# Wide side products from contiguous forms, and the fourth weight sum on GpSimd, in a transformer kernel on one core

## The chip, the cores and the metric

The kernel runs on one core of a Trainium2 chip. The metric is the device time in microseconds (us) of one execution. Engines: PE is TensorE's matmul side and PEld its weight load, DVE is VectorE, ACT is ScalarE, POOL is GpSimd, SP is SyncE, which issues the loads of the weights.

## The reference

Two blocks of two layers each work on one sequence of 512 tokens with 1024 features, in fp32. They contain attention mixers and six gated feed-forward networks, and the change lies in the first half of these:

```python
gate, up = jnp.split(h @ w_ffn_in[l], 2, axis=-1)      # first block
f = (jax.nn.silu(gate) * up) @ w_ffn_out[l]
...
return (jax.nn.silu(h @ wg) * (h @ wu)) @ wd           # second block
```

`h` is x after an RMS norm, 512 x 1024; gate and up have 2816 columns, which are 22 tiles of 128.

## The kernel before

**Precision.** Each fp32 operand is split into a high part (rounded to fp32r by ScalarE) and a low part (the rest). A product is three matmuls: high weight by high data, high weight by low data, low weight by high data. Weights are stationary, the data moves through, 512 columns of tokens at most.

**Order of work.** Weights come in units of 128 x 1024 floats through a ring of four slots (`w_raw`, with `w_hi` and `w_lo` beside it). Each engine runs its own queue, written out by hand; semaphores with counted values join them. In most stages ScalarE makes a unit's high part, GpSimd the low part (`split`, L757 to L764).

**The pair stage.** Each of the six networks does its first 5 gate and 5 up tiles in the plain way (`PLAIN` is 10) and then 17 pairs of a gate tile and an up tile (`PAIRS_ST`) by Strassen's method in Winograd's form: the pair's weights are a 2 x 2 matrix of blocks (gate and up by the halves of the features, `A11`, `A12`, `A21`, `A22`), the data one of 2 x 2 "forms" of 4 x 256 columns a partition (`B11`, `B21`, ... and the combinations `T1` to `T4`). A pair needs seven products instead of eight, and four sums of weight blocks (`S1` to `S4`, each 128 x 512):

- S1 = A21 + A22 (`first_sum`, L1833), S2 = S1 + A11 (`second_sum`, L1837), S4 = S2 + A12 (`fourth_sum`, L1841), S3 = A11 + A21 (`third_sum`, L1845); the signs that the method needs lie in the forms and in `hidden`. All four are VectorE's additions, line L1825.
- The high parts of blocks and sums are ScalarE's (`high`, L1146), the low parts VectorE's (`low`, L1818). The low part of a sum is written over the sum.

**TensorE's queue for pair p** (`paired_units`, L2785 to L2851): the products A11 x B11, S1 x T1, A22 x T4 of the pair before (`fourth`), S2 x T2, A12 x B21, S4 x B22, S3 x T3, counted on `st_prod`. Each is 8 matmuls with the high weight (L2806, L2808) and 4 with the low weight (L2813), all 256 columns wide. Only A12 x B21 of pairs 1 to 15 (`st.wide(p)`) is different: B21's high and low parts lie in `mvh` in such a way that one matmul takes both, 512 columns as 2 pieces of 256 that are two tiles apart (L2803), so that 4 matmuls do for 8. Its halves land in the two halves of `left_bank`, and must be added later.

**VectorE's queue for pair p** (`period`, L1872 to L1932, with q = p + 1) in order: low part of A11 of pair q, S1, the product of SiLU(gate) and up of the pair before (`hidden`, L1854), low part of A22, S2, low parts of S1 and S3 together (128 x 1024), low part of A12; then, after product six and ScalarE's third copy, the gate's additions: L1917 (out of both banks, 512 columns), S4's sum, L1921 (the right half of `left_bank`, 256 columns); then `last_half` (L1869), S3's sum, low parts of S2 and S4 together.

**ScalarE's queue** (`period`, L1180): copies of partial results out of PSUM (L1189, `fifth_copy` L1163, `sixth_copy` L1172), the high parts in the order in which TensorE needs them, SiLU (L1168) after the gate's additions, and then S4's high part. In pair 0 the high part of form T3 (`form_high`, L1143) stands ahead of the fifth copy, and T4 behind it; T3's high part waits until VectorE has split B21 (`form_low`, L1814). TensorE waits for the fifth copy before it begins A12 x B21.

**GpSimd** has nothing to do during the pairs. Its next work are the splits of the stage that follows (`splits`, L779).

**SyncE** (`pairs`, L715) loads a pair's two units when the counts of `st_sum` and `st_lo` say that the slots are free.

Of the kernel before, what the change touches and what calls it, by code (L numbers as in the profile page):

```python
# [32 lines left out]
S = 512  # L33
# [104 lines left out]
def program(nc, x_in, p_in, weights, cols_in, gmlp_in, dist_in, ident_in, rotary_in,  # L138
# [4 lines left out]
    with ExitStack() as ctx:  # L143
# [434 lines left out]
        class Pairs:  # L578


            def __init__(self, name):
                L, i = lin[name], ffn_no(name)
                self.u0, self.e0, self.i = L.u0, L.e0, i
                self.f0 = FFN[name] + PLAIN // 2
                self.g0 = L.e0 + PLAIN
                self.sum0, self.hi0, self.lo0 = 4 * PAIRS_ST * i, (7 * PAIRS_ST + 4) * i, (7 * PAIRS_ST + 4) * i
                self.prod0, self.copy0, self.u_0 = (7 * PAIRS_ST + 3) * i, 3 * PAIRS_ST * i, PAIRS_ST * i
                self.slot0 = L.u0 + PLAIN
                self.form0 = 7 * i
                self.loads0 = (16 * ((PAIRS_ST + 1) // 2) * i, 16 * (PAIRS_ST // 2) * i)  # L590
                m = 4 if name[0] == "a" else 0
                wide = lambda t: t.rearrange("p a (b c) -> p (a b) c", c=S // 2)
                late = [wide(t[:, m + j:m + j + 2, :]) for t in (mvh, mvl) for j in (0, 2)]
                self.both = {B21: mvh[:, m:m + 4, :].rearrange("p (j a) (b c) -> p j (a b) c", j=2, c=S // 2)}

                def homes(y, big, scr):
                    ys = [wide(y[:, 2 * j:2 * j + 2, :]) for j in range(1, 4)]
                    tail = [wide(big[:, FT + 2 * j:FT + 2 * j + 2, :]) for j in range(3)]
                    return {B11: ys[0], T3: ys[1], T1: ys[2], B21: tail[0], B22: tail[1], T2: tail[2],
                            T4: wide(scr[:, 6:8, :])}  # L600

                self.full, self.low = homes(y, big, scr), homes(y_r, big_r, scr_r)
                tabs = [tab_r[:, 1024 * j:1024 * (j + 1)].rearrange("p (a c) -> p a c", c=S // 2) for j in range(2)]
                pair = lambda t: t.rearrange("p (s a) (b c) -> p s (a b) c", s=2, c=S // 2)
                self.normal = [pair(y[:, 2:6, :]), pair(big[:, FT:FT + 4, :])]
                self.high = {B11: wide(scr_r[:, 8:10, :]), T1: tabs[0], T2: tabs[1]}
                self.high.update({B21: late[0], B22: late[2], T3: self.low[B21], T4: self.low[B22]})
                self.low.update({B21: late[1], B22: late[3]})

            def block(self, of, form, n=1):  # L610
                at = (2 * (self.slot0 % RING) + form) % 8
# [22 lines left out]
            def wide(self, p):  # L634

                return 0 < p < PAIRS_ST - 1
# [119 lines left out]
        def _(pool):  # L756
# [19 lines left out]

            done = [0]

            def splits(until):  # L779

                u0 = done[0]
                turns = (until - u0) // RING
                if turns:
                    with pool.Fori(0, turns) as t:
                        for j in range(RING):
                            split(t * RING + u0 + j, (u0 + j) % RING)
                for u in range(u0 + turns * RING, until):
                    split(u, u % RING)
                done[0] = until
# [195 lines left out]
        def _(act):  # L985
# [143 lines left out]
            def ffn_in(name):  # L1129
# [50 lines left out]
                def period(t, p):  # L1180
                    q = p + 1
                    product_done(t, p, 1)
                    if p == 0:
                        act.wait_ge(hidden_ready, st.f0 - 1)
                    elif p == 1:
                        act.wait_ge(hidden_ready, st.f0)
                    else:
                        ge(act, bank_free, t * 2 + st.g0 + p - 1)
                    nc.scalar.activation(parted[:, (p + 1) % 2, 0:S // 2], st.chain_bank(p)[:, 0:S // 2],  # L1189
                                         ACT.Copy).then_inc(st_copy, 1)  # L1190
                    if p == 1:
                        silu_pair(t, 0)
                        sum_high(t, 1, S4)
                    if p == 0:
                        form_high(T3)
                        fifth_copy(t, p)
                        form_high(T4)
                    else:
                        sum_high(t, p, S3)
                    if q < PAIRS_ST:  # L1200
                        raw_high(t, q, A11, 0, 0)
                    if p:
                        fifth_copy(t, p)
                    if p == 0:
                        sixth_copy(t, p)
                    if p == 1:
                        product_done(t, p, 3)
                        raw_high(t, p, A22, 1, 1)
                    if q < PAIRS_ST:
                        sum_high(t, q, S1)  # L1210
                    else:
                        down_cast(2)
                    if p > 1:
                        product_done(t, p, 3)
                    if p != 1:
                        raw_high(t, p, A22, 1, 1, 1 if q < PAIRS_ST else 3)
                    if p:
                        sixth_copy(t, p)
                    if q < PAIRS_ST:
                        sum_high(t, q, S2)  # L1220
                        product_done(t, p, 5)
                        raw_high(t, q, A12, 0, 1)
                    else:
                        down_cast(3)
                        down_high(name, 0)
                    if p:
                        silu_pair(t, p)
                        if q < PAIRS_ST:
                            sum_high(t, q, S4)
                    if q == PAIRS_ST - 1:  # L1230
                        act.wait_ge(mv_free, st.i + 1)
                        down_cast(0)
                        down_cast(1)
# [397 lines left out]
        def _(dve):  # L1631
# [150 lines left out]
            def ffn_in(name):  # L1782
# [41 lines left out]
                def summed(t, q, form, a, b):  # L1824
                    nc.vector.tensor_tensor(st.sum(form), a, b, ALU.add).then_inc(st_sum, 1)  # L1825

                def sum_ready(t, q, n):
                    dve.wait_ge(st_sum, t * 8 + st.sum0 + 4 * q + n)
# [9 lines left out]
                    sum_ready(t, q, 1)  # L1838
                    summed(t, q, S2, st.sum(S1), st.raw(q, 0, 0))

                def fourth_sum(t, q):  # L1841
                    sum_ready(t, q, 2)
                    summed(t, q, S4, st.sum(S2), st.raw(q, 0, 1))

                def third_sum(t, q):  # L1845
                    summed(t, q, S3, st.raw(q, 0, 0), st.raw(q, 1, 0))

# [24 lines left out]
                def period(t, p):  # L1872
# [41 lines left out]
                    if st.wide(p):  # L1914
                        halves = lambda a: a.rearrange("p (j c) -> p j c", j=2)
                        g, b = halves(g1[:, p % 2, :]), halves(parted[:, (p + 1) % 2, :])
                        nc.vector.tensor_tensor(g, st.sides(p, 0), b, ALU.add).then_inc(gate_begun, 1)  # L1917
                        fourth_sum(t, q)
                        dve.wait_ge(gate_begun, t * 2 + (PAIRS_ST - 2) * st.i + p)
                        gate = g1[:, p % 2, 0:S // 2]  # L1920
                        nc.vector.tensor_tensor(gate, st.left_bank(p)[:, S // 2:S], gate, ALU.add).then_inc(bank_free, 1)  # L1921
                    else:
                        nc.vector.tensor_tensor(g1[:, p % 2, :], st.side_bank(p)[:, :], parted[:, (p + 1) % 2, :],
                                                ALU.add).then_inc(bank_free, 1)
                        if more:
                            fourth_sum(t, q)
                    if p:
                        last_half(t, p)
                    if more:
                        third_sum(t, q)  # L1930
                        high_ready(t, q, 7)
                        low(S2, st.sum(S2, 2), 2, 2)  # L1932
# [643 lines left out]
        def _(pe):  # L2576
# [208 lines left out]
            def paired_units(name):  # L2785
# [3 lines left out]
                def product(t, p, bank, weight, n_hi, n_lo, form, begin, more=1):  # L2789
# [6 lines left out]
                    high, low = st.high[form], st.low[form]  # L2796
                    both = st.both[form] if form in st.both and st.wide(p) else None
                    if both is not None:
                        whole = bank
                    for k in range(4):  # L2800
                        w = st.hi(weight)[:, k * P:(k + 1) * P]
                        if both is not None:
                            nc.tensor.matmul(whole.rearrange("p (j c) -> p j c", j=2), w, both[:, :, k, :],  # L2803
                                             start=(begin and k == 0), stop=False, skip_group_check=True)
                            continue
                        nc.tensor.matmul(bank, w, high[:, k, :], start=(begin and k == 0), stop=False,  # L2806
                                         skip_group_check=True)
                        nc.tensor.matmul(bank, w, low[:, k, :], start=False, stop=False, skip_group_check=True)  # L2808
                    pe.wait_ge(st_lo, t * 14 + st.lo0 + 7 * p + n_lo)
                    bank = bank[:, 0:S // 2] if both is not None else bank  # L2810
                    for k in range(4):
                        w = st.lo(weight)[:, k * P:(k + 1) * P]
                        last = nc.tensor.matmul(bank, w, high[:, k, :], start=False, stop=(k == 3),  # L2813
# [12 lines left out]
                def period(t, p):  # L2826
                    chained, left, right = st.chain_bank(p)[:, 0:S // 2], st.side_bank(p)[:, 0:S // 2], st.right(p)
                    fifth_at, third_at = right, right
                    if st.wide(p):
                        left = st.left_bank(p)[:, :]  # L2830
                    if p == 1:
                        pe.wait_ge(bank_free, st.g0)
                    elif p:
# [872 lines left out]
```

## Time and profile before

| | us |
|---|---|
| median of 3 runs | 3206.0 |
| lowest and highest run | 3204.86 and 3206.11 |
| the profiled execution | 3205.18 |
| its span, first to last instruction | 3203.4 |
| TensorE busy | 3154.3 |
| VectorE busy | 2038.4 |
| ScalarE busy | 1497.2 |
| GpSimd busy | 1096.5 |

The span is that of the profiled execution, and the time of that execution is 1.8 us longer. The granted clock of TensorE was 0.999 of full speed over the span. Busy times are sums over instructions of one engine; on VectorE, ScalarE and TensorE an instruction can start before the one ahead of it has ended, so two starts are a better measure of a step than a duration. Starts are in us from the span's start.

### The profile page before, as it was taken

What the parts mean: (1) busy time and instruction counts of PE and PEld (TensorE: products, weight loads), DVE (VectorE), ACT (ScalarE), POOL (GpSimd) and SP (SyncE); (2) the same over time, 40 slices, a digit from 0 to 9 for tenths busy, and PEclk for the clock granted to TensorE, in tenths of its full rate; (3) what the DMA queues carried; (4) which work ended last, traced back from release to release, by engine and by line L of the source; (5) the groups of instructions that cost most, each with busy time, mean ns of one, the idle gap of its engine ahead of it and who ended that gap; (6) DMA issues with size and microseconds to landing.
All of it is one profiled execution on the core that took longest, in us unless ns stands there. A gap on an engine that the chain in (4) does not pass through costs nothing.

```text
span 3203.4 us, 53431 instructions
## 1 busy us (share of the span) xinstructions
PE 3154.3 (98%) x18866; PEld 2726.9 (85%) x18866; DVE 2038.4 (64%) x3193; ACT 1497.2 (47%) x2696; POOL 1096.5 (34%) x635
## 2 busy tenths in 40 slices
PE   9999999999999999999999999999999999999999
PEld 7678998786689987899888778998899887789987
DVE  4748884558488845888445247874698443348854
ACT  4655552547555524555333434552355333335542
POOL 5533014765340146500465341014400453350034
PEclk9999999999999999999999999999999999999999
DMA  4112332221123322222422122232222322122231
GB/s 158 53 47 86 106 117 99 86 103 53 47 85 106 112 103 81 80 105 92 154 92 86 53 73 79 105 118 98 79 101 92 130 93 71 61 86 92 105 119 66
DMA packets 82432, 294.25 MB, mean 92 GB/s; under 512 B 9035, under 2 KB 11467, under 8 KB 82028
## 3 DMA queue, kind: packets, MB, share of 16 engines
q1 hardware_dynamic: 80944, 286.06, 25.4%
q10 hardware_dynamic: 1340, 6.23, 0.5%
q8 instruction: 92, 1.51, 0.2%
q14 instruction: 56, 0.46, 0.0%
HBM read 290.15 MB, written 2.10 MB: 91 GB/s over the span
## 4 chain that ended last, share of the span: by engine, by line
PE 90%; DVE 4%; issue 2%; POOL 2%; ACT 2%; DMA 0%; SPq 0%; POOLq 0%; DVEq 0%; ACTq 0%
PE bank L2581 17%; PE bank L2582 17%; PE bank L2583 17%; PE bank L2813 10%; PE bank L2806 9%; PE bank L2808 9%; PE bank L2803 3%; PE bank L3215 1%; PE bank L3195 1%; POOL w_lo L762 1%; DVE w_lo L1818 1%; PE bank L3302 1%; POOL diag L897 1%; PE bank L3057 1%; PE bank L3337 0%
## 5 line engine op out<-in xcount | busy, mean ns | idle before, releaser
L762 POOL TENSOR_TENSOR w_lo<-w_raw,w_hi 128x1024 fp32r<-128x1024 f32 (+1 forms) x334 | 790.5, 2375 | 1852.2 <-ACT w_hi L991 1808.1
L2581 PE MATMUL bank<-mvh,w_hi 128*128 128x512 f32 (+1 forms) x2774 | 1056.9, 381 | 10.1 <-DVE mvl L1727 2.9
L2583 PE MATMUL bank<-mvh,w_lo 128*128 128x512 f32 (+1 forms) x2774 | 1034.5, 373 | 0.0
L2582 PE MATMUL bank<-mvl,w_hi 128*128 128x512 f32 (+1 forms) x2774 | 1033.8, 373 | 0.0
L991 ACT ACTIVATE w_hi<-w_raw 128x1024 fp32r<-128x1024 f32 x333 | 350.9, 1058 | 799.7 <-PE bank L2583 759.3
L2581 PEld LDWEIGHTS bank<-mvh,w_hi 128*128 128x128 f32 x2774 | 522.5, 188 | 135.3 <-issue 35.2
L2583 PEld LDWEIGHTS bank<-mvh,w_lo 128*128 128x128 f32 x2774 | 522.3, 188 | 93.6
L2582 PEld LDWEIGHTS bank<-mvl,w_hi 128*128 128x128 f32 x2774 | 523.1, 189 | 84.4 <-issue 0.2
L1992 DVE TENSOR_TENSOR mvl<-big,mvh 128x512 fp32r<-128x512 f32 x108 | 255.3, 2364 | 327.8 <-ACT mvh L1280 327.8
L1146 ACT ACTIVATE w_hi<-w_lo_as 128x512 fp32r<-128x512 f32 x408 | 254.7, 626 | 202.8 <-DVE w_lo_as L1825 202.8
L2808 PE MATMUL bank<-y_as,w_hi 128*128 128x256 f32 x1224 | 306.9, 283 | 0.0
L1818 DVE TENSOR_TENSOR w_lo<-w_lo_as,w_hi 128x1024 fp32r<-128x1024 f32 (+1 forms) x216 | 251.1, 1165 | 42.7 <-ACT w_hi L1146 33.5
L1818 DVE TENSOR_TENSOR w_lo<-w_raw,w_hi 128x512 fp32r<-128x512 f32 x306 | 210.8, 689 | 52.7 <-ACT w_hi L1146 49.6
L2808 PEld LDWEIGHTS bank<-y_as,w_hi 128*128 128x128 f32 x1224 | 235.0, 192 | 0.2
L2806 PE MATMUL bank<-tab_as,w_hi 128*128 128x256 f32 x816 | 204.6, 283 | 0.0
L2806 PE MATMUL bank<-big_as,w_hi 128*128 128x256 f32 x816 | 204.6, 283 | 0.0
L1146 ACT ACTIVATE w_hi<-w_raw 128x512 fp32r<-128x512 f32 x306 | 189.1, 618 | 2.3 <-issue 2.3
L1168 ACT ACTIVATE scr<-scr 128x512 f32<-128x512 f32 x102 | 64.5, 632 | 222.8 <-DVE scr L1921 211.1
L897 POOL TENSOR_TENSOR diag<-diag,scr 128x512 f32<-128x512 f32 (+1 forms) x144 | 160.5, 1115 | 19.0 <-ACT scr L1009 3.3
L2806 PEld LDWEIGHTS bank<-big_as,w_hi 128*128 128x128 f32 x816 | 156.6, 192 | 0.2
L2806 PEld LDWEIGHTS bank<-tab_as,w_hi 128*128 128x128 f32 x816 | 156.7, 192 | 0.0
L1825 DVE TENSOR_TENSOR w_lo_as<-w_lo_as,w_raw 128x512 f32<-128x512 f32 x204 | 139.4, 683 | 6.9 <-PE bank L2583 6.1
(301 smaller groups left out, 4941.9 us busy)
## 6 DMA issues: line engine op xcount, KB each, us to landing
w_raw<-in_weights SPq DMA_DIRECT2D x537, 512.0 KB, 3.2
x<-in_x SPq DMA_DIRECT2D x8, 256.0 KB, 7.8
out_y<-y SPq DMA_DIRECT2D x8, 256.0 KB, 2.2
tab<-in_dist ACTq DMA_DIRECT2D x2, 640.0 KB
tab<-in_gmlp ACTq DMA_DIRECT2D x2, 640.0 KB
tab<-in_ret_dil ACTq DMA_DIRECT2D x1, 1280.0 KB
y<-in_p ACTq DMA_DIRECT2D x2, 512.0 KB, 3.4
y<-in_rotary ACTq DMA_DIRECT2D x1, 1024.0 KB
```

Source lines behind the costliest of these rows:

```text
L762: last = nc.gpsimd.tensor_tensor(w_lo[:, slot, at], w_raw[:, slot, at], w_hi[:, slot, at].bitcast(F32), ALU.subtract)
L897: nc.gpsimd.tensor_tensor(at, at, sq_at(name, i), ALU.add).then_inc(sq_used, 1)
L991: nc.scalar.activation(w_hi[:, slot, :], w_raw[:, slot, :], ACT.Copy).then_inc(w_hi_ready, 1)
L1146: nc.scalar.activation(st.hi(form), src, ACT.Copy).then_inc(st_hi, more)
L1818: nc.vector.tensor_tensor(st.lo(form, n), src, st.hi(form, n).bitcast(F32), ALU.subtract).then_inc(st_lo, more)
L1992: nc.vector.tensor_tensor(mvl[:, slot0 + s % 4, :], src, mvh[:, slot0 + s % 4, :].bitcast(F32), ALU.subtract).then_inc(mv_lo, 1)
L2581: nc.tensor.matmul(bank[:, at], hi, mvh[:, k, at], start=first, stop=False, skip_group_check=again)
L2582: nc.tensor.matmul(bank[:, at], hi, mvl[:, k, at], start=False, stop=False, skip_group_check=again)
L2583: return nc.tensor.matmul(bank[:, at], lo, mvh[:, k, at], start=False, stop=last, skip_group_check=again)
L2806: nc.tensor.matmul(bank, w, high[:, k, :], start=(begin and k == 0), stop=False, skip_group_check=True)
L2808: nc.tensor.matmul(bank, w, low[:, k, :], start=False, stop=False, skip_group_check=True)
L2813: last = nc.tensor.matmul(bank, w, high[:, k, :], start=False, stop=(k == 3), skip_group_check=True)
```

## The change

Four things change.

1. The forms B21 and B22 lie differently in `mvh` and `mvl`: for each of the four k, high part and low part are side by side, 256 and 256 columns. B22's product becomes a wide one too, and both wide products read 512 contiguous columns. S4 x B22 lands in both halves of `side_bank`.
2. The gate's second addition therefore takes the right halves of both banks, 512 columns instead of 256. It follows the first one directly.
3. S4's sum is taken out of VectorE's queue and given to GpSimd (`fourth_sums`), which waits for S2's sum and for the sixth product of the pair before. VectorE waits for it ahead of S3's sum. `splits` calls it when it passes the units of a pair stage.
4. In pair 0 ScalarE makes the fifth copy ahead of form T3's high part.

```diff
-                late = [wide(t[:, m + j:m + j + 2, :]) for t in (mvh, mvl) for j in (0, 2)]
-                self.both = {B21: mvh[:, m:m + 4, :].rearrange("p (j a) (b c) -> p j (a b) c", j=2, c=S // 2)}
+                self.both = {B21: mvh[:, m:m + 4, :], B22: mvl[:, m:m + 4, :]}
+                split = lambda t, j: t.rearrange("p k (j c) -> p j k c", j=2)[:, j]
...
-                self.high.update({B21: late[0], B22: late[2], T3: self.low[B21], T4: self.low[B22]})
-                self.low.update({B21: late[1], B22: late[3]})
+                self.high.update({B21: split(self.both[B21], 0), B22: split(self.both[B22], 0), T3: self.low[B21], T4: self.low[B22]})
+                self.low.update({B21: split(self.both[B21], 1), B22: split(self.both[B22], 1)})
...
+            def fourth_sums(name):
+
+                st = Pairs(name)
+
+                def body(t, q):
+                    pool.wait_ge(st_sum, t * 8 + st.sum0 + 4 * q + 2)
+                    pool.wait_ge(st_prod, t * 14 + st.prod0 + 7 * (q - 1) + 6)
+                    nc.gpsimd.tensor_tensor(st.sum(S4), st.sum(S2), st.raw(q, 0, 1), ALU.add).then_inc(st_sum, 1)
+
+                body(0, 1)
+                pair_loop(pool, 2, PAIRS_ST, body)
+
             def splits(until):
+
+                for name in FFN:
+                    pairs_at = lin[name].u0 + PLAIN
+                    if done[0] <= pairs_at < until:
+                        plain_splits(pairs_at)
+                        fourth_sums(name)
+                plain_splits(until)
+
+            def plain_splits(until):
...
                     if p == 0:
+                        fifth_copy(t, p)
                         form_high(T3)
-                        fifth_copy(t, p)
                         form_high(T4)
...
                         nc.vector.tensor_tensor(g, st.sides(p, 0), b, ALU.add).then_inc(gate_begun, 1)
-                        fourth_sum(t, q)
                         dve.wait_ge(gate_begun, t * 2 + (PAIRS_ST - 2) * st.i + p)
-                        gate = g1[:, p % 2, 0:S // 2]
-                        nc.vector.tensor_tensor(gate, st.left_bank(p)[:, S // 2:S], gate, ALU.add).then_inc(bank_free, 1)
+                        nc.vector.tensor_tensor(g, st.sides(p, 1), g, ALU.add).then_inc(bank_free, 1)
                     else:
                         nc.vector.tensor_tensor(g1[:, p % 2, :], st.side_bank(p)[:, :], parted[:, (p + 1) % 2, :],
                                                 ALU.add).then_inc(bank_free, 1)
-                        if more:
-                            fourth_sum(t, q)
                     if p:
                         last_half(t, p)
                     if more:
+                        sum_ready(t, q, 3)
                         third_sum(t, q)
...
-                        whole = bank
+                        whole, bank = bank, bank[:, 0:S // 2]
                     for k in range(4):
                         w = st.hi(weight)[:, k * P:(k + 1) * P]
                         if both is not None:
-                            nc.tensor.matmul(whole.rearrange("p (j c) -> p j c", j=2), w, both[:, :, k, :],
-                                             start=(begin and k == 0), stop=False, skip_group_check=True)
+                            nc.tensor.matmul(whole, w, both[:, k, :], start=(begin and k == 0), stop=False, skip_group_check=True)
                             continue
...
-                        left = st.left_bank(p)[:, :]
+                        left, third_at = st.left_bank(p)[:, :], st.side_bank(p)[:, :]
```

## Rows read from the trace of the kernel before

**Rows 1.** The page, busy time of each engine over the whole span.

```profile
PE 3154.3 (98%) x18866; PEld 2726.9 (85%) x18866; DVE 2038.4 (64%) x3193; ACT 1497.2 (47%) x2696; POOL 1096.5 (34%) x635
```

**Rows 2.** Waits of the weight loads, whole span: total us, times, longest.

```profile
PEld bank L2806 <- ACT scr L1163: 7.3, 6, 1.2
...
PEld bank L2813 <- DVE w_lo L1818: 3.6, 12, 0.4
```

**Rows 3.** The chain that ended last, two wide products: start, us, what.

```profile
383.25 0.93 PE bank L2803 x4
393.28 0.93 PE bank L2803 x4
```

**Rows 4.** Timeline of VectorE, pairs 2 and 3: start, us, what, idle before.

```profile
327.05 0.68 DVE L1917 TENSOR_TENSOR scr<-bank,scr 128x512 f32<-128x512 f32 x1
...
328.25 0.41 DVE L1921 TENSOR_TENSOR scr<-bank,scr 128x256 f32<-128x256 f32 x1
...
334.31 0.69 DVE L1825 TENSOR_TENSOR w_lo_as<-w_lo_as,w_raw 128x512 f32<-128x512 f32 x1
335.10 1.23 DVE L1818 TENSOR_TENSOR w_lo<-w_lo_as,w_hi 128x1024 fp32r<-128x1024 f32 x1
336.25 0.68 DVE L1818 TENSOR_TENSOR w_lo<-w_raw,w_hi 128x512 fp32r<-128x512 f32 x1
336.85 0.68 DVE L1917 TENSOR_TENSOR scr<-bank,scr 128x512 f32<-128x512 f32 x1
```

**Rows 5.** Timeline of ScalarE, pair 2: SiLU and the high part of S4.

```profile
328.70 0.63 ACT L1168 ACTIVATE scr<-scr 128x512 f32<-128x512 f32 x1 [2.31 <-DVE scr L1921]
329.23 0.61 ACT L1146 ACTIVATE w_hi<-w_lo_as 128x512 fp32r<-128x512 f32 x1
```

**Rows 6.** Timeline of TensorE: product seven of pair 8, and the down stage.

```profile
385.92 0.28 PE L2806 MATMUL bank<-big_as,w_hi 128*128 128x256 f32 x1
...
386.88 0.64 PE L2813 MATMUL bank<-big_as,w_lo 128*128 128x256 f32 x4
...
479.69 0.39 PE L2582 MATMUL bank<-mvl,w_hi 128*128 128x512 f32 x1
...
485.81 0.39 PE L2582 MATMUL bank<-mvl,w_hi 128*128 128x512 f32 x1
```

**Rows 7.** Timeline of VectorE in pair 8: low part of A12, first gate addition.

```profile
385.56 0.68 DVE L1818 TENSOR_TENSOR w_lo<-w_raw,w_hi 128x512 fp32r<-128x512 f32 x1
386.22 0.69 DVE L1917 TENSOR_TENSOR scr<-bank,scr 128x512 f32<-128x512 f32 x1
```

**Rows 8.** GpSimd's groups by form: a 512-column addition (count, busy us, mean ns, idle).

```profile
L847 POOL TENSOR_TENSOR big<-big,scr 128x512 f32<-128x512 f32 x16 | 20.7, 1293 | 0.2
```

**Rows 9.** One VectorE line that reads PSUM, and GpSimd's splits beside some.

```profile
L1790 DVE TENSOR_TENSOR scr<-bank,rstd_b x60: 674/682/692, 262.9 to 2901.4; 128x512 f32<-128x512 f32 x60
...
265.32 9.96 POOL L762 TENSOR_TENSOR w_lo<-w_raw,w_hi 128x1024 fp32r<-128x1024 f32 x4 [1.51 <-ACT w_hi L991]
```

**Rows 10.** VectorE and GpSimd on two SBUF tensors each: a page group, then timelines.

```profile
L1992 DVE TENSOR_TENSOR mvl<-big,mvh 128x512 fp32r<-128x512 f32 x108 | 255.3, 2364 | 327.8 <-ACT mvh L1280 327.8
...
16.83 1.72 DVE L1713 SCALAR_TENSOR_TENSOR mvl<-x,cols,mvh 128x512 fp32r<-128x512 f32 x1
...
18.14 1.57 POOL L897 TENSOR_TENSOR diag<-diag,scr 128x512 f32<-128x512 f32 x1
21.56 1.57 POOL L897 TENSOR_TENSOR diag<-diag,scr 128x512 f32<-128x512 f32 x1
...
270.12 1.39 DVE L1800 SCALAR_TENSOR_TENSOR y<-x,cols,bank 128x512 f32<-128x512 f32 x2
```

**Rows 11.** Timeline of VectorE in pairs 0 and 1: second sum, low parts.

```profile
305.44 0.69 DVE L1825 TENSOR_TENSOR w_lo_as<-w_lo_as,w_raw 128x512 f32<-128x512 f32 x1
...
306.78 1.52 DVE L1818 TENSOR_TENSOR w_lo<-w_raw,w_hi 128x512 fp32r<-128x512 f32 x2
...
316.64 0.69 DVE L1818 TENSOR_TENSOR w_lo<-w_raw,w_hi 128x512 fp32r<-128x512 f32 x1 [0.49 <-ACT w_hi L1146]
```

More of the change, by code:

```diff
@@ L1839, in second_sum @@
                     summed(t, q, S2, st.sum(S1), st.raw(q, 0, 0))
-                def fourth_sum(t, q):
-                    sum_ready(t, q, 2)
-                    summed(t, q, S4, st.sum(S2), st.raw(q, 0, 1))
                 def third_sum(t, q):
@@ L2809, in product @@
                     pe.wait_ge(st_lo, t * 14 + st.lo0 + 7 * p + n_lo)
-                    bank = bank[:, 0:S // 2] if both is not None else bank
                     for k in range(4):
```

## The prediction

> **What bounds the kernel now.** The page's busy times come first: TensorE is busy 98% of the span [rows 1]. So a change must either shorten TensorE's own steps or leave another engine late enough to stop it. Next the list of waits of the weight loads (a matmul shows no idle time while its weight load waits): in the six pair stages only two waits repeat, on the fifth copy of pair 0 (6 times, 7.3 us) and on low weights from VectorE (12 times, 3.6 us, two a stage) [rows 2]. Then the chain around pair 8: its wide product starts again 10.03 us later, with nothing but matmuls in between [rows 3]. In the steady part the pair's 10.03 us are TensorE's own.
>
> The timeline tells how near VectorE is. Early in the stage it does not yet follow TensorE: from the first gate addition of pair 2 (L1917, 327.05) to that of pair 3 (336.85) it takes 9.80 us, though TensorE's period is 10.03 [rows 4]. That loop goes through ScalarE: both gate additions, SiLU, high part of S4 (L1168, L1146) [rows 5], VectorE's low part of S2 and S4, and so on to the low part of A12 (336.25) and the next gate addition. It holds almost no slack, only 0.23 us a period against TensorE, with which it wins back the lateness left by pair 0. In pair 8 it has done so: the gate addition starts at 386.22, just after TensorE went on to S3 at 385.92 [rows 6, 7]. Taken back five periods, that is 336.05 in pair 3, and VectorE came at 336.85, 0.8 us late. In pair 2, before TensorE's last stop, it was later still.
>
> **The change part by part.** Both wide products. A contiguous 512-column matmul starts every 0.2267 us (27 steps, 479.69 to 485.81); a 256-column one every 0.12 (385.92 to 386.88, 8 steps) [rows 6]. The strided one before takes 0.93 for four [rows 3]. B21 goes from 0.93 to 0.907, B22's high part from 0.96 to 0.907: 0.076 us a pair, on the path while TensorE bounds. With 15 wide pairs in each of 6 stages that is 6.9 us. Nothing shows that the contiguous read in this place is slower, but if it stays at 0.2325, 2.7 us are left.
>
> VectorE's side. The fourth sum (0.68, 0.60 to the next start) goes; the second gate addition grows from 256 to 512 columns, 0.41 to 0.69, and now waits at once for the first. A result passed on through a semaphore costs 0.79 from start to start (334.31 to 335.10). From the first gate addition to the end of the second were 1.61 us (327.05 to 328.66) and will be 0.79 + 0.69 = 1.48 [rows 4]: the loop falls from 9.80 to 9.67, unless GpSimd costs it something. The third sum now waits for GpSimd; beside additions out of PSUM it starts 0.79 + 0.60 + 0.33 = 1.7 us after the first, and GpSimd's 1.29 [rows 8] is over. At last, queued behind that wait are S3's sum and the low part of S2 and S4, which also waits for ScalarE; nothing is added.
>
> The fourth sum on GpSimd. It waits for S2's sum and for product six of the pair before. Where TensorE bounds, product six comes last, when the low part of A12 has held VectorE since 385.56 [rows 7], and the sum runs beside the gate additions. These read PSUM, and such additions are not slowed: 60 of L1790 took at most 692 ns, some under GpSimd's splits [rows 9]. Where VectorE is late, product six is long done and S2's sum starts GpSimd: exactly when the low part of S1 and S3 starts, then that of A12, and both read two SBUF tensors. Such work doesn't share: VectorE's subtractions of the down stage take 2364 ns on average [rows 10]; and where both queues were full, each VectorE instruction waited for one of GpSimd's, one GpSimd addition starting every 1.71 us (18.14, then 21.56 two later), where VectorE alone needs 0.66 (two in 1.39) [rows 10]. So one collision costs VectorE 1.71 - 0.66 = 1.05 us. The ends are 0.84 (half of 2.36 - 0.69, since a split has 1024 columns) and 1.29, GpSimd's whole unblocked instruction [rows 8]; I take 1.05, from the same pair of engines and the same size. The collision falls between second sum and gate addition, where the loop has no idle time. A late loop is then 9.67 + 1.05 = 10.72 us, more than TensorE's 9.95: it never catches up, stays late, and so collides in every pair.
>
> The Trainium skill (SBUF — State Buffer, section "Who interferes with whom") says that the pair of ports is held for the whole instruction, whichever engine issued first. By that 1.29 would count in place of 1.05 and the time would be 3289; the alternating rows favour the smaller figure.
>
> Start of a stage. Pair 0 is late because of the form splits, before any pair work. GpSimd's first sum is released by the second sum at 306.1 and falls among VectorE's low parts, where 0.15 us were idle (1.52 for two of 0.69): 0.9 us. In pair 1 an idle 0.49 and the 0.13 saved soften it: 1.05 - 0.49 - 0.13 = 0.43 [rows 11]. S4's sum leaves VectorE's queue there too, but SiLU and the high part still follow the gate addition, so nothing is won. The fifth copy ahead of form T3: ScalarE was idle before T3, so the copy is free and T3 is no later. The stop of 7.3 us / 6 = 1.2 us [rows 2] goes, but TensorE then meets the low part of S2 for pair 1, for which it already waited; late next is VectorE. I take nothing for it; the bounds are 0 and 7.3 us in all. Nothing changes on the queues: SyncE's weight loads wait for the same counts, GpSimd's splits of the down stage come after the last sum, and GpSimd was idle through the pairs. The strided reads of low products stay 256-column runs, costed at nothing.
>
> **Sum.** Each stage: 0.9 + 0.43 at the start, then 13 periods (pair 2 to pair 15) of 10.72 instead of 10.03: 9.0; together 10.3, and 6 stages make 62. Against the profiled execution's 3205.2 us that is 3267; its 3203.4 us span has 1.8 around it, and the median of the runs, 3206.0, stands 0.8 higher, which I leave out. The bounds of a collision move 15 of them a stage: 0.84 gives 3248, 1.29 gives 3289.
>
> **The rivals.** First, the placement works and TensorE stays the bound: **not slower**. The point that decides is whether GpSimd's request comes after the low part of A12 has begun, that is, whether VectorE is less than about 0.6 us late (386.22 - 385.56, less the 0.07 of shorter products). For it: the steady pairs are like that, and VectorE could keep the ports through instructions back to back, so that a waiting GpSimd gets them only at the gate addition. Against: pair 2 and 3 are later than that, and the alternating rows show GpSimd getting in between. Time: 3206 - 6.9 = 3199; with the whole stop at the fifth copy won 3192, with the strided price 3203.
>
> Second, collisions only in the first pairs, after which VectorE recovers, since a collision costs it under 0.28 us where part of it meets idle time. Three bad periods of 0.69 and the start of 1.3, less eleven periods of 0.076, are 2.6 us a stage: 3221. Against it: no idle time stands at that place.
>
> Third, the sum is slower on GpSimd than anything shown and holds up the third sum. Between 1.7 and 2.7 us after the first gate addition there is nearly 1 us before ScalarE's high part binds VectorE; even GpSimd's blocked 1.57 [rows 10] stays below. It adds no case of its own. That the change doesn't do what it says: a wide product at the strided pace, in the first rival.
>
> **How the numbers follow.** A measurement of this kernel tells about 0.2% (6.4 us) from no change. Late and colliding in every pair, 3267: 0.74. First rival, 3199: 0.19, half on either side of 0.2% (0.10 faster, 0.09 same). Second, 3221: 0.07. The range leaves out the first rival and reaches from below the second to the upper bound of a collision: 3212 to 3290. Slower is 0.74 + 0.07 = 0.81.
>
> **What would show it.** Right: the wide products start some 10.7 us apart; L1818 of 512 or 1024 columns lasts over 1 us longer in most pairs, while GpSimd's 96 sums start about at the end of S2's sum; weight loads of the low products wait for VectorE in nearly every pair; the loop's other steps are unchanged. Wrong: pairs 9.95 us apart, GpSimd's sums starting with the gate addition, L1818 still 0.69 and 1.22. Then the step that failed is the lateness or who gets the ports. If the collision shows but the pairs are 10.2 apart, its price was too high.

## The result and the profile after

The changed kernel took 3267.15 us (median of 4 runs, 3265.9 to 3267.63), the kernel before 3205.43 us beside it. The ratio is 1.0192, with a 95% interval of 1.018 to 1.0204: slower by some 62 us. The forecast was 3267.

The page of the changed kernel gives the busy time of the engines and two groups that tell most of it: GpSimd's new sum (L786) and VectorE's low parts of 512 columns (L1839, which was L1818). Columns of a group: count, busy us, mean ns, then the idle time ahead of it.

```profile
span 3265.8 us, 53011 instructions
PE 3180.7 (97%) x18506; PEld 2714.7 (83%) x18506; DVE 2104.7 (64%) x3097; ACT 1477.6 (45%) x2696; POOL 1307.9 (40%) x731
...
L786 POOL TENSOR_TENSOR w_lo_as<-w_lo_as,w_raw 128x512 f32<-128x512 f32 x96 | 210.9, 2197 | 923.4 <-PE bank L2825 674.1
...
L1839 DVE TENSOR_TENSOR w_lo<-w_raw,w_hi 128x512 fp32r<-128x512 f32 x306 | 311.7, 1020 | 67.2 <-ACT w_hi L1167 65.4
```

VectorE has 96 instructions fewer than in [rows 1] and is still busy for 66 us more. It did not get more work: its 90 wider second additions add less than the 96 sums that it gave away. The 306 low parts of one block last 1020 ns on average. Before they were 0.68 to 0.69 us wherever one stands alone [rows 4, 7, 11]. And a GpSimd addition, 1.29 us in [rows 8], is recorded with 2197 ns; the shortest of the 96 has 1707. Two engines got longer at once; e2 and e5 below show that the one causes the other.

The waits of the weight loads and of GpSimd's sums, total us, times and longest:

```profile
PEld bank L2825 <- DVE w_lo L1839: 50.0, 90, 0.7
...
PEld bank L2819 <- DVE bank L1886: 8.8, 6, 1.5
...
POOL w_lo_as L786 <- PE bank L2825: 674.1, 80, 8.5
```

The first two answer to [rows 2]. The wait for a low part came 12 times and comes 90 times now, once in every wide pair of every stage. The stop at the fifth copy is gone, and a new one of 1.5 us a stage stands five products later in TensorE's queue, ahead of A22 x T4 of pair 0, on `last_half` (L1886).

The timeline of VectorE in pairs 2 and 3 of the first stage, then GpSimd's and TensorE's in pair 3 (start, us, what, idle before):

```profile
329.74 0.68 DVE L1934 TENSOR_TENSOR scr<-bank,scr 128x512 f32<-128x512 f32 x1
330.45 0.69 DVE L1936 TENSOR_TENSOR scr<-bank,scr 128x512 f32<-128x512 f32 x1
...
336.80 0.68 DVE L1846 TENSOR_TENSOR w_lo_as<-w_lo_as,w_raw 128x512 f32<-128x512 f32 x1
337.59 1.23 DVE L1839 TENSOR_TENSOR w_lo<-w_lo_as,w_hi 128x1024 fp32r<-128x1024 f32 x1
338.73 1.77 DVE L1839 TENSOR_TENSOR w_lo<-w_raw,w_hi 128x512 fp32r<-128x512 f32 x1
340.42 0.68 DVE L1934 TENSOR_TENSOR scr<-bank,scr 128x512 f32<-128x512 f32 x1
...
468.61 0.68 DVE L1934 TENSOR_TENSOR scr<-bank,scr 128x512 f32<-128x512 f32 x1
...
337.65 2.29 POOL L786 TENSOR_TENSOR w_lo_as<-w_lo_as,w_raw 128x512 f32<-128x512 f32 x1 [8.39 <-PE bank L2825]
...
336.84 0.64 PE L2825 MATMUL bank<-mvl,w_lo 128*128 128x256 f32 x4
...
338.87 0.73 PE L2825 MATMUL bank<-big_as,w_lo 128*128 128x256 f32 x4 [0.43 <-DVE w_lo L1839]
```

Read it against [rows 4]. S2's sum ends at 337.48 (336.80 + 0.68). GpSimd starts at 337.65, when the low part of S1 and S3 (337.59) has begun. That one keeps its 1.23 us, and now the low part of A12 stands for 1.77 us instead of 0.68: GpSimd's turn comes between the two. From one gate addition to the next are 10.68 us. The last gate addition of the wide pairs, pair 15, comes at 468.61: (468.61 - 329.74) / 13 = 10.68 us again, so no pair gets better. TensorE does its 8 high matmuls of S3 and stops for the low part, which is late by the same rhythm.

TensorE's product six ends at 337.48 too (336.84 + 0.64), and the profile names it, not S2's sum, as what released 80 of the 96 sums. In these pairs product six ends with S2's sum or 0.2 us behind it. It is no earlier, because TensorE itself was stopped in the pair before by a late low part; the two engines are late together, and GpSimd's request always falls ahead of the low part of A12.

TensorE's timeline of both wide products in pair 8:

```profile
388.10 1.09 PE L2817 MATMUL bank<-mvh,w_hi 128*128 128x512 f32 x4
389.03 0.63 PE L2825 MATMUL bank<-mvh,w_lo 128*128 128x256 f32 x4
389.50 1.09 PE L2817 MATMUL bank<-mvl,w_hi 128*128 128x512 f32 x4
390.43 0.64 PE L2825 MATMUL bank<-mvl,w_lo 128*128 128x256 f32 x4
390.91 0.28 PE L2819 MATMUL bank<-big_as,w_hi 128*128 128x256 f32 x1
```

Four contiguous matmuls take 389.03 - 388.10 = 0.93 us, just what four strided ones took [rows 3]. The whole product takes 1.40 and 1.41 us.

### The profile page after: what moved, and what is told of

It reads as the page before. It is cut to its first block, busy times and chain, and to the rows that moved or that the text cites. A ratio compares the mean times of both kernels' runs of the same rounds, so it can differ in the third digit from the quotient of the medians.

```text
span 3265.8 us, 53011 instructions
## 1 busy us (share of the span) xinstructions
PE 3180.7 (97%) x18506; PEld 2714.7 (83%) x18506; DVE 2104.7 (64%) x3097; ACT 1477.6 (45%) x2696; POOL 1307.9 (40%) x731
## 4 chain that ended last, share of the span: by engine, by line
PE 71%; DVE 10%; issue 9%; ACT 5%; POOL 2%; DVEq 1%; ACTq 0%; DMA 0%; POOLq 0%; SPq 0%
PE bank L2595 17%; PE bank L2597 16%; PE bank L2596 16%; PE bank L2825 5%; ACT w_hi L1167 4%; PE bank L2819 3%; PE bank L2821 3%; DVE w_lo L1839 3%; DVE w_lo_as L1846 3%; PE bank L2817 1%; POOL diag L918 1%; DVE scr L1936 1%; DVE scr L1934 1%; PE bank L3227 1%; PE bank L3207 1%
## 5 line engine op out<-in xcount | busy, mean ns | idle before, releaser
L786 POOL TENSOR_TENSOR w_lo_as<-w_lo_as,w_raw 128x512 f32<-128x512 f32 x96 | 210.9, 2197 | 923.4 <-PE bank L2825 674.1
L1839 DVE TENSOR_TENSOR w_lo<-w_raw,w_hi 128x512 fp32r<-128x512 f32 x306 | 311.7, 1020 | 67.2 <-ACT w_hi L1167 65.4
L1839 DVE TENSOR_TENSOR w_lo<-w_lo_as,w_hi 128x1024 fp32r<-128x1024 f32 (+1 forms) x216 | 251.1, 1165 | 45.8 <-ACT w_hi L1167 36.6
L2825 PE MATMUL bank<-big_as,w_lo 128*128 128x256 f32 x816 | 139.3, 293 | 29.1 <-DVE w_lo L1839 29.1
```

The costliest lines, as they stand in the source:

```text
L786: nc.gpsimd.tensor_tensor(st.sum(S4), st.sum(S2), st.raw(q, 0, 1), ALU.add).then_inc(st_sum, 1)
L1839: nc.vector.tensor_tensor(st.lo(form, n), src, st.hi(form, n).bitcast(F32), ALU.subtract).then_inc(st_lo, more)
```

## The experiments

The theory: VectorE leaves the start of each stage late, so GpSimd's sum falls on low parts that read two SBUF tensors; the two take turns, one collision costs VectorE about 1.09 us (1.78 - 0.69), its loop with ScalarE becomes 10.68 us, longer than TensorE's 10.00, and so it stays late. The rivals: the new dependency (S3's sum waits for GpSimd) is what costs; the wide products or the wider second addition cost; GpSimd's waits by themselves cost. All times are medians; ratios are to the kernel before, run beside each on the same chip.

**e1, the sum back on VectorE.**

```diff
                         nc.vector.tensor_tensor(g, st.sides(p, 0), b, ALU.add).then_inc(gate_begun, 1)
+                        fourth_sum(t, q)
                         dve.wait_ge(gate_begun, t * 2 + (PAIRS_ST - 2) * st.i + p)
...
-                        sum_ready(t, q, 3)
                         third_sum(t, q)
...
-                        fourth_sums(name)
```

> The changed kernel with S4's sum back in VectorE's queue between the two gate additions (and after the one of pair 0); both wide products, the 512-column second addition and the order of the copies stay. If GpSimd's sum is the whole cost, the 61 us go. VectorE's loop is then 9.80 us as before plus 0.28 for the wider second addition, 10.08 us, against some 10.00 of TensorE in the changed kernel (the wide products kept their 0.93 us for four, so the two save only 0.03 us a pair): about 13 x 0.05 x 6 = 4 us over before, 3207 to 3212 us. Rival, the wide products or the wider addition are what costs: the time stays above 3240.

3210.36 us, ratio 1.0015 (1.0006 to 1.0024). Of the 62 us, 57 are gone with GpSimd's sum. What stays is the other half of this expectation: the first gate additions in the middle of the stage are 10.07 us apart, a little over TensorE's own pace.

```profile
387.82 0.68 DVE L1937 TENSOR_TENSOR scr<-bank,scr 128x512 f32<-128x512 f32 x1
389.02 0.69 DVE L1940 TENSOR_TENSOR scr<-bank,scr 128x512 f32<-128x512 f32 x1
...
397.89 0.69 DVE L1937 TENSOR_TENSOR scr<-bank,scr 128x512 f32<-128x512 f32 x1
```

So the second wide product without relief for VectorE is a small loss here: it puts 256 more columns into an addition on VectorE's loop.

**e2, the same sum, started later.** One wait is added, on the low part of A12 of the same pair.

```diff
                     pool.wait_ge(st_prod, t * 14 + st.prod0 + 7 * (q - 1) + 6)
+                    pool.wait_ge(st_lo, t * 14 + st.lo0 + 7 * q + 5)
```

> The changed kernel with one more wait ahead of GpSimd's sum: on the low part of A12 of the same pair. The sum then always starts when VectorE turns to the gate additions out of PSUM. Theory (two queues that both read two SBUF tensors take turns): no low part lasts longer than 0.69 or 1.23 us, VectorE's loop is 9.67 us, TensorE bounds again at about 10.00 us a pair, 3199 to 3205 us. Rival (the third sum waits for a slow GpSimd, and the dependency is the cost): starting the sum later makes it worse than 3267 us.

3201.55 us, ratio 0.9988 (0.9979 to 0.9997): faster than both kernels. The groups of low parts and of GpSimd's sum, the early gate additions on VectorE, and the chain:

```profile
L1840 DVE TENSOR_TENSOR w_lo<-w_raw,w_hi 128x512 fp32r<-128x512 f32 x306 | 211.1, 690 | 63.0 <-ACT w_hi L1168 61.4
...
L787 POOL TENSOR_TENSOR w_lo_as<-w_lo_as,w_raw 128x512 f32<-128x512 f32 x96 | 124.2, 1294 | 947.7 <-DVE w_lo L1840 828.3 <-PE bank L2826 119.4
...
325.73 0.68 DVE L1935 TENSOR_TENSOR scr<-bank,scr 128x512 f32<-128x512 f32 x1
326.45 0.69 DVE L1937 TENSOR_TENSOR scr<-bank,scr 128x512 f32<-128x512 f32 x1
...
335.32 0.69 DVE L1935 TENSOR_TENSOR scr<-bank,scr 128x512 f32<-128x512 f32 x1
...
381.80 0.93 PE bank L2818 x4
383.20 0.93 PE bank L2818 x4
391.80 0.93 PE bank L2818 x4
```

The same 96 additions last 1294 ns instead of 2197, and the low parts are back at 690. A later start makes it 66 us faster, so a dependency on a slow GpSimd is not the cause (the times are medians: 3267.15 and 3201.55). The loop without a collision is 335.32 - 325.73 = 9.59 us, and TensorE's own pair 391.80 - 381.80 = 10.00. The difference between 9.59 and the 10.68 of the changed kernel is 1.09, the excess of one low part.

**e3, GpSimd's sum alone.** The kernel before with `fourth_sums` and `sum_ready(t, q, 3)` as in the change, and `fourth_sum` taken out of VectorE's queue.

> The kernel before with S4's sum given to GpSimd with the change's two waits, and nothing else of the change. Theory: the loop is 9.80 less 0.60 for the sum plus about 0.19, since the second addition (still 256 columns) now waits at once for the first, plus 1.09 of a collision: 10.48 us. It is 0.2 shorter than in the changed kernel for the narrower second addition: (10.48 - 10.03) x 13 x 6 = 35 us and about 8 at the starts: 3245 to 3255 us. Rival (the wide products take part in the cost): near 3206 or near 3267.

3244.13 us, ratio 1.012 (1.0105 to 1.0136). Its low part of A12 and the first gate additions of two pairs:

```profile
389.90 1.78 DVE L1839 TENSOR_TENSOR w_lo<-w_raw,w_hi 128x512 fp32r<-128x512 f32 x1
391.61 0.68 DVE L1934 TENSOR_TENSOR scr<-bank,scr 128x512 f32<-128x512 f32 x1
...
402.02 0.68 DVE L1934 TENSOR_TENSOR scr<-bank,scr 128x512 f32<-128x512 f32 x1
```

The lower end was 3245, so it was missed by 1 us: the loop is 10.42 us on average over the stage and not 10.48, since two gate additions that follow each other are 0.72 us apart (e2, 325.73 to 326.45), not 0.79. The sum alone makes the kernel slower, by 39 us; the wide products aren't needed for it. The other 23 of the 62 come with the rest of the change, most of them with the wider second addition: its loop of 10.68 against 10.42 makes 13 x 0.26 x 6 = 20. Alone, in e1, the wide products cost only 5, because there the loop's slack against TensorE took up most of it.

**e4, the order of the copies alone.**

```diff
                     if p == 0:
+                        fifth_copy(t, p)
                         form_high(T3)
-                        fifth_copy(t, p)
                         form_high(T4)
```

> The kernel before with only the fifth copy of pair 0 ahead of form T3. I took nothing for it: TensorE's stop of 1.2 us per stage at the fifth copy goes, and it stops as much longer at the low part of S2 in pair 1, where it already waited for VectorE. Theory: within 1.5 us of before. Rival (the stop is worth what it lasts): 7 us faster, 3199 us.

3204.53 us, ratio 0.9997 (0.9988 to 1.0006), no difference that can be told. Its waits of the weight loads show why:

```profile
PEld bank L2813 <- DVE w_lo L1818: 6.5, 12, 0.7
...
PEld bank L2806 <- DVE bank L1869: 3.6, 6, 0.6
```

Before they were 7.3 and 3.6 us [rows 2], 10.9 together; now 3.6 and 6.5, 10.1 together. TensorE stops as long, at another place.

**e5, e6 and e7, an addition for nobody.** The kernel before, all of its work unchanged, with an additional x + x on GpSimd where the change has its sum; 512, 256 and 8 columns.

```diff
+                    pool.wait_ge(st_sum, t * 8 + st.sum0 + 4 * q + 2)
+                    pool.wait_ge(st_prod, t * 14 + st.prod0 + 7 * (q - 1) + 6)
+                    ge(pool, extra, t * 2 + 16 * st.i + q - 1)
+                    nc.gpsimd.tensor_tensor(scr[:, 4, 0:512], x[:, 0, 0:512], x[:, 1, 0:512], ALU.add).then_inc(extra, 1)
```

> The kernel before, unchanged on its four other engines, and an additional addition on GpSimd at the place of the change's (same two waits): x + x, 512 columns, into a free part of scr, for which nobody waits. No dependency is added, only the use of SBUF by a second engine. Theory (the queues take turns): VectorE's loop is 9.80 + 1.09 = 10.89 us, 0.86 over TensorE's 10.03; 13 x 0.86 x 6 = 67 us and 9 to 12 at the starts: 3278 to 3290 us. Rival (the cost lies in the new dependencies): 3206 us.

> As the run with 512 columns, but 256 columns. Theory: the collision costs half, about 0.55 us, the loop is 10.35 us: 13 x 0.32 x 6 = 25 us and 3 to 6 at the starts: 3231 to 3240 us. It is not in proportion to the work, since the first 0.23 us of each pair are free. If the loss did not depend on the length (an exchange between the queues costs a fixed time) it would be as with 512 columns.

> As the run with 512 columns, but 8 columns. Theory: a collision of less than 0.23 us, the slack of VectorE's loop against TensorE: VectorE catches up as before, 3205 to 3208 us. If GpSimd's waits or the exchange itself cost something, it would be seen here by itself.

| columns | us | ratio (95% interval) |
|---|---|---|
| 512 | 3286.71 | 1.0253 (1.0236 to 1.027) |
| 256 | 3233.53 | 1.0088 (1.0071 to 1.0105) |
| 8 | 3205.45 | 1.0 (0.9991 to 1.001) |

VectorE's timeline, the low part of A12 and the gate addition behind it, twice with 512 columns:

```profile
382.90 1.78 DVE L1840 TENSOR_TENSOR w_lo<-w_raw,w_hi 128x512 fp32r<-128x512 f32 x1
384.60 0.68 DVE L1939 TENSOR_TENSOR scr<-bank,scr 128x512 f32<-128x512 f32 x1
...
395.50 0.68 DVE L1939 TENSOR_TENSOR scr<-bank,scr 128x512 f32<-128x512 f32 x1
```

and the same with 256 columns:

```profile
388.41 1.22 DVE L1840 TENSOR_TENSOR w_lo<-w_raw,w_hi 128x512 fp32r<-128x512 f32 x1
389.56 0.68 DVE L1939 TENSOR_TENSOR scr<-bank,scr 128x512 f32<-128x512 f32 x1
...
399.89 0.68 DVE L1939 TENSOR_TENSOR scr<-bank,scr 128x512 f32<-128x512 f32 x1
```

Nobody waits for this addition, and it costs 81 us. The price follows the columns: 1.78 - 0.69 = 1.09 us for 512, 1.22 - 0.69 = 0.53 for 256, and the loops are 10.90 and 10.33 us, that is 9.80 plus the price. But the total doesn't follow them: half of the columns cost 28 us, a third of 81, since the first 0.23 us of each period (10.03 - 9.80) were free. With 8 columns (mean record 353 ns) even the collisions of the late pairs are absorbed; waits and exchange cost nothing that can be told. This also shows that lateness alone does no lasting harm: a collision smaller than the slack lets VectorE catch up, its early periods of 9.80 us going over into 10.03.

**e8, the additional wait in the first half only.** Pairs 1 to 9 are gated as in e2, pairs 10 to 16 are as in the change.

```diff
-                body(0, 1)
-                pair_loop(pool, 2, PAIRS_ST, body)
+                body(0, 1, True)
+                pair_loop(pool, 2, 10, lambda t, q: body(t, q, True))
+                pair_loop(pool, 10, PAIRS_ST, body)
```

> The changed kernel with the additional wait on the low part of A12 only for the sums of pairs 1 to 9 of each stage; pairs 10 to 16 have the change's own two waits. Theory (there are two steady states, and only the late start puts the kernel into the bad one): VectorE has caught up by pair 9, GpSimd's later sums wait for product six, which comes when the low part of A12 has begun, and nothing collides: 3200 to 3204 us. Rival (the change's waits always lead to collisions, late start or not): the second half loses (10.68 - 10.00) x 6 pairs x 6 = 24 us, 3224 to 3228 us.

3200.64 us, ratio 0.9985 (0.9976 to 0.9995). A low part of A12 near the end of the stage, GpSimd's sums there and their whole group:

```profile
444.84 0.68 DVE L1842 TENSOR_TENSOR w_lo<-w_raw,w_hi 128x512 fp32r<-128x512 f32 x1
...
445.50 1.30 POOL L788 TENSOR_TENSOR w_lo_as<-w_lo_as,w_raw 128x512 f32<-128x512 f32 x1 [8.71 <-PE bank L2828]
455.57 1.29 POOL L788 TENSOR_TENSOR w_lo_as<-w_lo_as,w_raw 128x512 f32<-128x512 f32 x1 [8.78 <-PE bank L2828]
...
L788 POOL TENSOR_TENSOR w_lo_as<-w_lo_as,w_raw 128x512 f32<-128x512 f32 x96 | 124.4, 1296 | 946.6 <-PE bank L2828 514.2 <-DVE w_lo L1842 432.4
```

The late sums carry exactly the change's two waits, are released by TensorE's product six and last 1.30 us. So the placement of the change is right for a VectorE that keeps up, and the kernel stays in that state once it is in it. In pairs 10 to 16 instructions and waits are those of the changed kernel, and their periods are 10.00 us instead of 10.68: two steady states exist for them, and what came before chooses. How many of the first pairs must be kept free of collisions was not tried; here it was nine.

**e9, the gated kernel with strided forms.**

```diff
-                self.both = {B21: mvh[:, m:m + 4, :], B22: mvl[:, m:m + 4, :]}
-                split = lambda t, j: t.rearrange("p k (j c) -> p j k c", j=2)[:, j]
+                apart = lambda t: t[:, m:m + 4, :].rearrange("p (j a) (b c) -> p j (a b) c", j=2, c=S // 2)
+                self.both = {B21: apart(mvh), B22: apart(mvl)}
+                split = lambda t, j: t[:, j]
```

> The gated kernel with both wide products reading two pieces of 256 columns that lie two tiles apart, as B21's did before, instead of 512 contiguous ones. In the changed kernel the contiguous ones took the same 0.93 us for four as the strided ones before. Theory (the layout buys nothing here): the same time as the gated kernel, 3200 to 3203 us, pairs 10.00 us apart. Rival (a contiguous read is cheaper, 0.907 us for four, and something else hid it): 2 x 0.023 x 90 = 4 us more.

3201.49 us, ratio 0.9988 (0.9979 to 0.9997); e2 had 3201.55. The contiguous layout buys nothing that can be measured.

**e10, the gated kernel with the old order of the copies.** The reverse of e4's edit, in e2.

> The gated kernel with form T3's high part ahead of the fifth copy of pair 0 again. The order alone, in the kernel before, moved the time by 1.0 us or less. In the gated kernel VectorE leaves the start of a stage about 1.3 us earlier, so TensorE could use an early fifth copy. Theory (part of the stop of 1.2 us a stage is now worth something): 1 to 5 us slower than the gated kernel. Rival (VectorE's form splits bound the start here too): no difference.

3202.05 us, ratio 0.9989 (0.998 to 0.9998), half a microsecond above e2 and so below the expected 1 to 5. The intervals of the two overlap nearly whole: an effect of the order is not shown. The wait on the fifth copy is back in its profile (7.3 us, 6 times) with 2.4 us on the low parts, 9.7 together; e2 has 5.2 on the low parts and 3.6 on `last_half`, 8.8 together.

**e11, the kernel before with the gated sum.** e3 with e2's line.

> The kernel before with S4's sum on GpSimd behind all three waits, and nothing else of the change: narrow B22, old order of the copies. Against the gated kernel it lacks the second wide product, which saves 0.03 us a pair, 2.7 us in all. VectorE's loop is 9.59 less 0.28 = 9.3 us, so it catches up in two pairs. Theory: 3203 to 3206 us. Rival (all of the gain of the gated kernel comes from the sum on GpSimd): as fast as the gated kernel, 3201 us.

3202.88 us, ratio 0.9992 (0.9983 to 1.0001), 0.1 us below the expected range and some 1.3 us above e2, which has the second wide product and the new order besides. The interval holds 1, no change at all, and it overlaps e2's: about 2.5 of e2's 4 us seem to come from the moved sum, and how the gain is divided isn't shown.

## Why the prediction was right

**The price of a collision.** Taken as 1.71 - 0.66 = 1.05 from two queues that alternated; it is 1.09. Both bounds held: 0.84 from the down stage was too low, 1.29 too high. The 0.66 was read from two instructions that take one operand out of PSUM [rows 10]; by the 0.60 of this loop's own steps it would have been 1.11, nearer still. The Trainium skill (SBUF — State Buffer, section "Who interferes with whom") has the loser blocked for the whole instruction of the other. The runs show that it is blocked (e5 changed nothing but this), for 1.09 us of the 1.29 that GpSimd's record shows.

**The loop.** 9.67 + 1.05 = 10.72 was forecast, 9.59 + 1.09 = 10.68 measured. The 0.08 is mostly the step from one gate addition to the next, taken as 0.79 from another pair of instructions and measured as 0.72.

**Lateness and order.** That GpSimd gets its turn between two of VectorE's instructions, ahead of the low part of A12, is the row at 338.73. In all six stages the low part of A12 lasts 1.77 or 1.78 us in pairs 2 to 15 and 1.21 in pair 1; in pair 0 it is A22's that is longer. That the change's waits do no harm when VectorE is on time is e8. One step of the mechanism was wrong without harm to the number: product six was said to be long done in the late state, with S2's sum as the releaser. It ends at the same time as S2's sum or 0.2 us later, since TensorE is held in every pair by the low part of S3. The wide products start 10.5 and 10.9 us apart in turn, 10.68 on average, where one distance of 10.7 was named; why they alternate was not looked into. The first rival (VectorE keeps up) described the gated kernel: forecast 3199 with 3192 to 3203, measured 3201.6. It failed for the changed kernel at the point named, since VectorE is late in pair 2 in every stage.

**The start.** Forecast 0.9 and 0.43 us. VectorE's timeline of pairs 0 and 1:

```profile
307.25 2.39 DVE L1839 TENSOR_TENSOR w_lo<-w_raw,w_hi 128x512 fp32r<-128x512 f32 x2
...
317.92 1.21 DVE L1839 TENSOR_TENSOR w_lo<-w_raw,w_hi 128x512 fp32r<-128x512 f32 x1 [0.49 <-ACT w_hi L1167]
```

Two low parts take 2.39 where they took 1.52 [rows 11], 0.87 more. The idle time between the two was taken as 0.15 and was 0.22 (two without idle time take 0.61 + 0.69), so a price that was too small by 0.04 and an idle time too small by 0.07 nearly cancelled. Further, in pair 1 one takes 1.21 instead of 0.69, 0.52 more, of which a shorter way through the gate additions gives some back.

**The sum.** In the first stage TensorE needs 181.5 us from its first pair product to the down stage (297.05 to 478.58), before 171.3 (296.50 to 467.84): 10.2 more where 10.3 was forecast; six stages make 61. The parts lie differently. From pair 2's first wide product to pair 15's TensorE needs 8.0 us more, not 9.0 (one of the thirteen periods before lasted 10.44 and not 10.03, with TensorE's last stop in it); up to pair 2 it is 0.8, not 1.3, and behind pair 15 another 1.4, for which the sum had no term. That the total meets the measured one within 0.1 us is partly luck.

**What was off.** The wide products: the term took 0.907 us for four contiguous matmuls from the down stage, they take 0.93 in this place. So the saving is 0.02 to 0.03 us a pair, not 0.076; at 0.03 it is the 2.7 us in all that the text gave for this case. It did not enter the predicted time, since TensorE does not bound in the late state, but it made the gain of the first rival too large: 6.9 us where e2 shows 4, the moved sum included. The order of the copies was taken at nothing, and e4 agrees, with the mechanism as forecast: the wait moved to VectorE's low part, and also to `last_half`, which the text did not name. Last, that a matmul shows no idle time while its weight load waits is too strong: of the stop at 338.87 the matmul's row shows 0.43 us.

## What to carry to other kernels

When work moves from a full engine to an idle one, ask for each of its instructions what the first engine does at that moment, and release it by the event that makes the moment safe (here the end of the last low part), not by the data alone. A loop of one engine with little slack against another (0.23 us in 10.03 before, 0.41 in 10.00 with the change) has two steady states when being late makes it longer by more than that slack; with less, as in e7, it recovers. A placement that is right in the middle of a stage must also be checked in its first pairs, because they can decide which state the stage stays in.

## What the runs showed of the hardware that was not expected

- A GpSimd addition of two SBUF tensors delayed a VectorE subtraction of two by 1.09 us at 512 columns and 0.53 at 256, about 2.1 ns a column, with no fixed part to be seen; gate additions that read PSUM kept their 0.68 us beside it (e2).
- Four 512-column matmuls took 0.93 us in the wide products, contiguous (e2) or in two pieces (e9), while in the down stage one starts every 0.2267 us [rows 6], 0.907 for four. The layout is not the reason. What is was not tried.
- VectorE's step over its own semaphore was 0.72 us between the two additions out of PSUM (e2) and 0.79 between S2's sum and the next low part [rows 4], against 0.60 with no wait (e5, 384.60 and 385.20).
